# Values as the stationary operand in the first attention, with the head norm moved to features

## The reference, cut to what matters

```python
def diff_attend(q, k, v, lam):
    s = jnp.einsum('bqhmd,bkhmd->bhmqk', q, k).astype(jnp.float32) * (A_QK ** -0.5)
    p = jax.nn.softmax(s, axis=-1)
    a = p[:, :, 0] - lam * p[:, :, 1]
    return jnp.einsum('bhqk,bkhd->bqhd', a, v.astype(jnp.float32))

def diff_attention_post(o, subln, lam_init):
    B, N = o.shape[:2]
    return (rms_norm(o, subln) * (1.0 - lam_init)).reshape(B, N, BRANCH_W)
```

## Time and profile before

| | us |
|---|---|
| median of 3 runs | 1638.16 (1636.99 to 1640.24) |
| profiled execution | 1639.87 |
| its span in the profile | 1638.1 |
| TensorE busy, of the span | 1544.1 (94%) |
| VectorE | 759.3 (46%) |
| ScalarE | 670.9 (41%) |
| mean granted clock of TensorE | 0.982 |

### The profile page before, as it was taken

One profiled execution on the slowest core, in us unless ns is written; L12 is line 12 of the kernel. 1 busy time (PEld: TensorE's weight loads), 2 busy tenths in 40 slices (PEclk: granted clock), 3 DMA queues, 4 the chain that ended last, 5 costly groups with the idle time before them and its releaser, 6 DMA issues. The chain is left out here.

```text
span 1638.1 us, 29736 instructions
## 1 busy us (share of the span) xinstructions
PE 1544.1 (94%) x12509; PEld 1321.2 (81%) x12509; DVE 759.3 (46%) x1252; ACT 670.9 (41%) x1094; POOL 415.8 (25%) x107
## 2 busy tenths in 40 slices
PE   5999999999999999998989999977979999999998
PEld 4888898888888888987879887847868888888786
DVE  5344236678685510137854424458664333433002
ACT  5301325666643321137744534362354444344112
POOL 1222211111150243230022432200034343444342
PEclk9999999999999999999999999979999999999999
DMA  9344462253140032055221441000021232222321
GB/s 377 113 153 155 164 171 70 72 119 77 55 163 15 32 123 77 27 165 143 47 103 34 147 138 52 1 0 3 4 105 52 103 102 102 100 81 76 129 88 67
DMA packets 32598, 155.76 MB, mean 95 GB/s; under 512 B 6744, under 2 KB 8280, under 8 KB 18016
## 3 DMA queue, kind: packets, MB, share of 16 engines
q1 hardware_dynamic: 31456, 153.83, 28.4%
q10 hardware_dynamic: 1024, 0.21, 0.1%
HBM read 132.01 MB, written 2.10 MB: 82 GB/s over the span
## 5 line engine op out<-in xcount | busy, mean ns | idle before, releaser
L215 PE MATMUL banks<-ffn_token_parts,ffu_weight_parts 128*128 128x512 f32 (+1 forms) x1056 | 229.6, 380 | 1.2 <-POOL ffu_weight_parts L196 0.9
L215 PEld LDWEIGHTS banks<-ffn_token_parts,ffu_weight_parts 128*128 128x128 f32 x1056 | 191.7, 188 | 38.9 <-POOL ffu_weight_parts L196 1.1
L196 POOL TENSOR_TENSOR even_weight_parts<-weight_chunk,even_weight_parts 128x2048 fp32r<-128x2048 f32 x15 | 69.9, 4663 | 325.2 <-ACT even_weight_parts L190 325.2
L196 POOL TENSOR_TENSOR ffu_weight_parts<-weight_chunk,ffu_weight_parts 128x2048 fp32r<-128x2048 f32 x22 | 101.6, 4620 | 157.3 <-ACT ffu_weight_parts L190 157.3
L215 PE MATMUL banks<-even_token_parts,even_weight_parts 128*128 128x512 f32 (+1 forms) x672 | 124.8, 346 | 0.0
L940 PE MATMUL banks<-even_token_parts,even_weight_parts 128*128 128x512 f32 (+1 forms) x576 | 124.4, 351 | 0.0
L3156 PE MATMUL banks<-ffd_weight_parts,ffn_f_parts 128*128 128x512 f32 x528 | 120.1, 389 | 1.6 <-PEq L3057 1.6
L215 PEld LDWEIGHTS banks<-even_token_parts,even_weight_parts 128*128 128x128 f32 x672 | 103.6, 189 | 19.4 <-issue 3.8
L3156 PEld LDWEIGHTS banks<-ffd_weight_parts,ffn_f_parts 128*128 128x128 f32 x528 | 99.0, 188 | 22.5 <-issue 2.0
L215 PE MATMUL banks<-sec_token_parts,sec_weight_parts 128*128 128x512 f32 (+1 forms) x528 | 115.9, 377 | 0.3 <-PEq L283 0.3
L3134 DVE SCALAR_TENSOR_TENSOR ffn_conv<-banks,b_ffn_taps,ffn_conv 128x511 f32<-128x511 f32 (+1 forms) x88 | 61.9, 744 | 111.9 <-ACT ffn_conv L3106 108.8
(11 more groups left out here) (459 smaller groups left out, 2871.8 us busy)
## 6 DMA issues: line engine op xcount, KB each, us to landing
weight_chunk<-in_ffn_up SPq DMA_DIRECT2D x22, 1024.0 KB, 4.8
weight_chunk<-in_w_in_even SPq DMA_DIRECT2D x16, 1024.0 KB, 7.2
front_late<-in_w_mod SPq DMA_DIRECT2D x16, 1024.0 KB, 5.0
weight_chunk<-in_w_in SPq DMA_DIRECT2D x13, 1024.0 KB, 4.9
weight_chunk<-in_w_out SPq DMA_DIRECT2D x12, 1024.0 KB, 5.4
weight_chunk<-in_w_in_odd SPq DMA_DIRECT2D x12, 1024.0 KB, 4.8
weight_chunk<-in_ffn_down SPq DMA_DIRECT2D x11, 1024.0 KB, 4.8
front_w<-in_w_mod SPq DMA_DIRECT2D x8, 1024.0 KB, 22.9
```

The source lines that it names most:

```text
L196: self.nc.gpsimd.tensor_tensor(parts[:, 1], self.env.raw[s][:], parts[:, 0].bitcast(F32), ALU.subtract).then_inc(self.lo_done, 1)
L215: m = self.nc.tensor.matmul(o, w, env.tok[:, tp, k, a:b], start=n == 0, stop=n == 3 * KD - 1)
```

## The change

- `pv` works on pairs of query tiles. The values are the stationary operand (128x64) and `atT` moves, 128 columns. The two tiles of a pair write to partitions 0 to 63 and 64 to 127. A pair stands in the odd half-step of every second unit. The query order is now 0, 1, 4, 5, 2, 3.
- `out` copies a pair, without scaling, to `OT`, which has features on partitions.
- The first sums go to `sum_zero`, which is kept for all units. VectorE makes EPS * sum^2 of it at the end.
- ScalarE squares `OT` in four pieces behind units 40, 42, 44 and 49. TensorE makes the means over a head by products with `head_mean` (32 wide, four column groups) and adds EPS * sum^2 by products with the identity: `head_means`. ScalarE takes the root of 128x768, VectorE inverts it (128x768), and TensorE spreads the rows over the 64 partitions of a head: `spread`. VectorE multiplies (`normed_head`) and gates (`gate_head`).
- The 24 transposes at the end go. One half-step is now issued for each 8 of work, and the list of units is one shorter. SyncE no longer waits for `o_out` before it reloads x and ctx.

```diff
     SPLITS = 15, 16, 17, 18
+    SQUARES = 40, 42, 44, 49
...
-        issued = lambda work: 2 * LED - 1 + work * 2 // 15
+        issued = lambda work: 2 * LED - 1 + work // 8
...
+        spread_banks = (4, 0, 2, 4)
...
-            hh, qt = u // NT, (0, 1, 4, 2, 3, 5)[u % NT]
+            hh, qt = u // NT, (0, 1, 4, 5, 2, 3)[u % NT]
...
-                sp.wait_ge(o_out, UNITS)
...
+                def pv(p):
+                    hh, _, _, kts = unit(2 * p)
+                    pe.wait_ge(turned_out, 2 * p + 2)
+                    if p:
+
+                        pe.wait_ge(o_out, p)
+                    for i, kt in enumerate(kts):
+                        for j in range(2):
+                            r = nc.tensor.matmul(
+                                env.PS[j * A_V : (j + 1) * A_V, O0 + (p % 2) * P : O0 + (p % 2 + 1) * P],
+                                vN[:, kt, hh * A_V : (hh + 1) * A_V], atT[j][:, i * P : (i + 1) * P], start=i == 0, stop=i == len(kts) - 1)
                     r.then_inc(pv_ready, 1)
...
-                        if u >= 3:
-                            pv(u - 3)
+                        if u >= 3 and u % 2:
+                            pv((u - 3) // 2)
...
+                def head_means():
+                    pe.wait_ge(turned_out, UNITS)
+                    pe.wait_ge(o_out, PAIRS)
+                    pe.wait_ge(mean_made, 5)
+                    pe.wait_ge(bias_made, 1)
+                    pe.wait_ge(squared, FT)
+                    for a, b in ((0, S), (S, ST)):
+                        for f in range(FT):
+                            nc.tensor.matmul(env.PS[32 * f : 32 * (f + 1), T0 + a : T0 + b], head_mean[:], head_sq[:, f, a:b], start=True, stop=False)
+                    for t in range(NT):
+                        for f in range(FT):
+                            columns = sum_zero[:, sum_column(2 * f, t) : sum_column(2 * f, t) + 32]
+                            m = nc.tensor.matmul(
+                                env.PS[32 * f : 32 * (f + 1), T0 + t * P : T0 + (t + 1) * P], columns, env.ident[:], start=False, stop=t in (TX - 1, NT - 1))
+                    m.then_inc(o_mean, 1)
+
+                def spread(f):
...
+                    rows = slice(32 * f, 32 * f + 2)
+                    for j, (a, b) in enumerate(((0, S), (S, ST))):
+                        for h in range(2):
+                            pick = env.ident[rows, 32 * f + h : 32 * f + h + 1].to_broadcast([2, A_V])
...
+                                pick, root[rows, a:b], start=True, stop=True)
+                    m.then_inc(spread_ready, 1)
...
+                            if (n, c, k) == (TILES - 2, 1, 0):
+                                gate_row(0)
+                            if (n, c, k) == (TILES - 2, 1, 4):
+                                head_means()
+                            for g, at in enumerate((1, 2, 3, 5)):
+                                if (n, c, k) == (TILES - 1, 0, at):
+                                    spread(g)
+                            for g in (1, 2):
+                                if (n, c, k) == (TILES - 1, 0, 5 + g):
                                     gate_row(g)
...
+                def out(p):
+                    hh = unit(2 * p)[0]
+                    act.wait_ge(pv_ready, p + 1)
+                    for j in range(2):
+                        qt = unit(2 * p + j)[1]
+                        m = nc.scalar.copy(
+                            OT[hh % 2 * A_V : (hh % 2 + 1) * A_V, hh // 2, qt * P : (qt + 1) * P],
+                            env.PS[j * A_V : (j + 1) * A_V, O0 + (p % 2) * P : O0 + (p % 2 + 1) * P])
+                    m.then_inc(o_out, 1)
...
-                for s in range(2):
-                    out_ring.hi(act, 0, s)
+                out_ring.hi(act, 0, 0)
                 act.wait_ge(o_mean, 1)
-                nc.scalar.activation(head_ss[:], head_ss[:], ACT.Sqrt).then_inc(o_root, 1)
...
+                nc.scalar.activation(root[:], env.PS[:, T0 : T0 + ST], ACT.Sqrt).then_inc(o_root, 1)
+                out_ring.hi(act, 0, 1)
...
                 dve.wait_ge(o_root, 1)
-                st.link(nc.vector.reciprocal(head_ss[:], head_ss[:]))
...
+                nc.vector.reciprocal(root[:], root[:]).then_inc(inverted, 1)
+                for f in range(FT):
+                    normed_head(f)
+                for f in range(FT - 1):
+                    gate_head(f)
                 gate_row(1)
+                x_evacuated(TILES - 1)
                 gate_row(2)
...
+                gate_head(FT - 1)
```

More of the change, by code:

```diff
@@ L945, in _ @@
                                 work = (n - EARLY) * (X_WORK + C_WORK) + c * X_WORK + (2 - c) * (3 * k + i + 1)
-                                if half < 2 * (UNITS + 3) and half <= issued(work):
+                                if half < 2 * (UNITS + 2) and half <= issued(work):
                                     half_step(half)
                                     half += 1
-                            for g, at in enumerate(((TILES - 2, 0, 6), (TILES - 2, 1, 4), (TILES - 1, 0, 6))):
-                                if (n, c, k) == at:
-                                    gate_row(g)
[L952 to L962, removed]
+                            if (n, c, k) == (TILES - 2, 1, 0):
[7 more added lines that the diff above has]
+                                if (n, c, k) == (TILES - 1, 0, 5 + g):
+                                    gate_row(g)
             @block.scalar
@@ L1030, in exp_zero @@
                 def exp_zero(u):
-                    _, _, n, _ = unit(u)
+                    hh, qt, n, _ = unit(u)
+                    column = sum_column(hh, qt)
                     if u >= 2:
@@ L1036, in exp_zero @@
                     nc.scalar.activation(
-                        ex_zero[u % 2][:, 0:n], score(0, n), ACT.Exp, bias=neg_max[:, 0:1], accum_out=sums[:, u % 2, 0:1]).then_inc(exp_done[0], 1)
+                        ex_zero[u % 2][:, 0:n], score(0, n), ACT.Exp, bias=neg_max[:, 0:1],
+                        accum_out=sum_zero[:, column : column + 1]).then_inc(exp_done[0], 1)
                 def exp_one(u):
@@ L1045, in exp_one @@
                     nc.scalar.activation(
-                        ex_one[:, 0:n], score(1, n), ACT.Exp, bias=neg_max[:, 1:2], accum_out=sums[:, u % 2, 1:2]).then_inc(exp_done[1], 1)
+                        ex_one[:, 0:n], score(1, n), ACT.Exp, bias=neg_max[:, 1:2], accum_out=sum_one[:, u % 2 : u % 2 + 1]).then_inc(exp_done[1], 1)
                 def copy_out(u):
@@ L1051, in copy_out, with square @@
                     if u >= 2:
-                        act.wait_ge(pv_ready, u - 1)
+                        act.wait_ge(pv_ready, u // 2)
                     nc.scalar.copy(atT[u % 2][:, 0:n], env.PS[:, T0 : T0 + n]).then_inc(turned_out, 1)
[L1056 to L1061, removed]
+                def out(p):
[7 more added lines that the diff above has]
+                    m.then_inc(o_out, 1)
+                def square(f):
+                    act.wait_ge(o_out, 2 * HEAD_PAIRS * (f + 1))
+                    if f == 0:
+                        for s in range(2):
+                            act.wait_ge(stacked[s], 16 * 8 * 4)
+                    nc.scalar.activation(head_sq[:, f, :], OT[:, f, :], ACT.Square).then_inc(squared, 1)
                 def unit_steps(u):
@@ L1067, in unit_steps @@
                         exp_zero(u)
-                    if u >= 3:
-                        out(u - 3)
+                    if u >= 3 and u % 2:
+                        out((u - 3) // 2)
                     if u < UNITS:
@@ L1092, in _ @@
                 ring.hi(act, EVEN_EARLY // 2 + 1, 1, (v_ready, 2 * NT))
-                for u in range(LED, UNITS + 3):
+                for u in range(LED, UNITS + 2):
                     unit_steps(u)
+                    if u in SQUARES:
+                        square(SQUARES.index(u))
                     if u in SPLITS:
```

97 lines of the change are left out of this document (52 added, 45 removed).

## The result

| | median | lowest to highest | runs |
|---|---|---|---|
| before | 1636.34 us | 1629.97 to 1642.48 | 20 |
| changed | 1640.83 us | 1636.49 to 1648.77 | 20 |

The ratio of the changed kernel to the one before is 1.0037, 95% interval 1.0024 to 1.005: 4 to 8 us slower, and 4.5 us between the medians. The forecast was 4.5 us slower. The profiled execution has a span of 1640.9 us, against 1638.1.

A forecast was written before the change was run, and what follows sets the result against it. TensorE was taken to bound the first attention stage, with the softmax chain some 0.3 us behind. The terms -6 + 5.5 - 1.5 - 1 - 1.8 + 9.7 = +4.9, counted as +4.5, gave 1642.7 us, range 1638 to 1647.

The forecast's parts named there:

- The units, work: First attention's units: two long ones take 8.80 us; -6 us over seven heads, -1 for the fourth unit.
- The rival in which TensorE stays the bound: At the value pair's wait for the copy: TensorE still bounds the units; 1631 us (1628 to 1634), chance 0.2.
- The units, waits: ScalarE's extra work behind even units' exps delays the pair: 13 us of waits instead of 7.4, +5.5.
- the 7 that I had named as a sign of being wrong: Value pair's wait for the copy: forecast wrong if it stays at 7 us and units come every 3.5 us.
- The units, clock: Lower TensorE clock in the units, 7.0 us lost before: -1.5 us (bounds -5 and +3).
- The end, clock: Slow stretch after TensorE's wait for the root's inverse: 1.7 us lost (bounds 0 and 3.4).
- the pair's rate: Spreads at the end, priced like the value pair: 1.35 us each, 1.55 with entering and leaving; four take 6.2.
- The end, the rest: After the last value products: products and gate rows 18.5, head means 3.0, spreads 6.2, wait 4.0, last tile 3.9 us.
- Squares and tables: Squares between exps: six table loads, 7.7 us on ScalarE; 1650 us; chance 0.1 together with non-overlapping head means or spreads.
- The sum: Whole attention stage: -6 + 5.5 - 1.5 - 1 - 1.8 + 9.7 = +4.9 us, counted as +4.5.
- eight bigger ones: ScalarE's head splits, conv bases and squares behind even units' exps, each near 0.9 us.
- the 23 us by the factor of two: Value products of eight heads: saving by the factor alone, a pair at 1.35 us; 20 by the trace was taken.

The follow-up runs named there:

- cut_after: Changed kernel with both maxima of a long unit taken over the first 256 of its 768 columns; 1625.73 us, 0.9929 of before.
- filled: Changed kernel with gate rows 1 and 2 moved ahead of the first spread, into the wait for the inverse; spreads keep 2 rows; 1634.33 us.
- both: Changed kernel with spreads over 128 rows and both gate rows moved into the wait for the inverse; 1624.01 us, 0.9942 of before; again 1627.28 us.
- odd: Kernel of both with the first three squares behind units 41, 43, 45 instead of 40, 42, 44; 1630.53 us, again 1624.92 us.
- full_rows: Changed kernel with every product of a spread over all 128 rows instead of 2; 1631.64 us, 0.998 of before.

## Why the prediction was right, and where its terms were not

**The units, work.** Right. A long pair takes 1.47 us (337.63 to 339.10; 1.55 forecast), a short one 0.59 (0.70). The cycles are 8.74, 6.85 and 7.32 us, where I had 8.80, 6.65 and 6.98; the head 22.9, where I had 22.4. The Trainium skill, "TensorEngine Tiling (Array Packing)", Overview, promises up to 2x for 64 columns; the pair against two of the old blocks (2.70) is 1.8x here, the idle 0.17 us behind it included. The rival in which TensorE stays the bound is refuted by `cut_after`: shorten the chain, and 11.9 us appear.

**The units, waits.** The size was right (idle +5.2, +5.5 forecast), the place only in part. I had put the waits on the copy alone, 12 us or more; it has 7.5, close to the 7 that I had named as a sign of being wrong. The combining ahead of it has 5.9, where it had 1.9. Both are links of one chain. I had followed it only at its last link, while the transposes can already be late.

**The units, clock.** Mis-sized. I took -1.5 us, with bounds -5 and +3. It was -7.0, all that the earlier trace rows showed as lost, outside even my bounds (13.7 us at half clock cost 6.8; 7.0 is by the rounded shares of the earlier trace rows). Then -10.4 = +5.0 idle - 7.0 clock - 8.4 work, against +5.5 - 1.5 - 7.0. Three profiles of the old form have the slow stretches, and eight of ten of the new have none. Which part of the edit removes them (the values as the stationary operand, the order of units or the pace) wasn't tried. So two thirds of what the units won is clock, and its cause is not shown.

**The end, clock.** Mis-sized by far more than any other term. I took one slow stretch worth 1.7 us, bounds 0 and 3.4, from what followed a wait of 2.8 us in the earlier trace rows. It was 23.9 us at half clock, 11.9 us lost. The wait did start it, as I had put it: the clock fell at 448.86 us, within the wait, and with 128 rows it stayed up only when the wait was gone. That the spreads' products would keep the clock down was no term at all: I priced them by the pair's rate at full clock, 1.55 us each. At full clock each took 1.5 with 2, 32 or 128 rows; at half clock it took 2.8, with 2 rows or 128.

**The end, the rest.** Right. Without the clock term I had 37.3 - 1.7 = 35.6 us; the measured end less half its slow stretch is 34.3 to 34.9 in the kernels with the wait. Of that, head means 2.7 (3.0 forecast), wait for the inverse 3.3 (4.0), spreads at full clock 5.8 (6.2), products, gate rows and the last tile 22.5 (18.5 + 3.9). The reciprocal took 4.95 us (5.0), worked out from 6.4 ns a column. With the gate rows ahead of the spreads the end is 32.1 to 32.5, so at full clock the wait was worth 2.4 us (34.9 against 32.5) and had cover waiting for it.

**Squares and tables.** No table load stands between an exp and a square (L1106 is at 837 ns, idle 0.0). That rival is out.

**The sum.** The clock gave 5.5 us more than I had in the units and took 10.2 more at the end; work gave 1.4 more in the units and 1.2 more behind them, the rest of the end 1.2 (9.7 + 10.2 - 18.7), and the waits 0.5. That is 10.2 - 5.5 - 4.3 = +0.4, and unit 4 started 0.4 later: 4.9 became 5.7. The verdict was right because two errors in one kind of term had opposite signs. That is luck. The mechanism that was forecast, a chain that binds the units and an end that gets longer, is what the runs show. Two slips changed nothing in the sum: the "eight bigger ones" are seven in the list that is added up, and the 23 us by the factor of two leave the short pairs at 0.70 us; with the factor there too it is 25.

## What to carry to other kernels

Price a new TensorE block at both clocks, and ask of each block how many rows its products use: a broadcast of one or two rows took the same time over all 128, against zeros (1.51 us a spread, 1.50 over 2 rows). The rows that are not wanted must hold finite numbers, as they do here, because they are multiplied by zero. Here that alone was worth 7 to 8 us of the end behind the wait and 4.7 without it, and, with the idle time before it filled, turned a loss of 0.4% into a gain of 0.6%. Before products leave an engine that is at 96%, chain the next engine's path link by link; what it doesn't let through comes back as waits in small pieces, at several instructions. Place long instructions of a second engine behind the units whose result is not asked for next.

## What the hardware did that I had not expected

- TensorE's clock fell to 1.2 GHz while it was busy for 14.05 of 14.24 us, with products over 2 rows among them, and stayed there while busy for 10.24 of 10.24 (`filled`). The same schedule over 128 rows stayed at 2.4 GHz (`both`, and again in `both_again`, `odd` and `odd_again`); 32 rows gave 3.4 us.
- The two causes together give more than their sum: the wait alone gave 6.8 us at half clock (`full_rows`), the 2 rows alone 10.2 (`filled`), in one execution of each; together 20.5 and 23.9. `cut_after` has 23.9 too, and an end of 46.2 us.
- Slow stretches of 10.2 to 13.7 us in the units, where the old form was busy for 95 to 96% of the time, are gone in eight of ten profiles of the new one, which idles more (7%). In both forms a fall came only behind a wait of 1.5 us or more. Why the waits of 1.7 to 1.8 us in the new form were so rarely followed by one stays open.
